# Seven-product matrix blocks in the last layer of a four-layer forward pass, with edits at the joins of its stages

## The reference

```python
proj = h @ w_in[l]
rq, rk, rv, rg, mq, mk, mv, ga, gb = jnp.split(proj, split_points, axis=-1)
rq = rotary(rq.reshape(B, S, RET_HEADS, RET_DK), pos)
rk = rotary(rk.reshape(B, S, RET_HEADS, RET_DK), pos) * (RET_DK ** -0.5)
rv = rv.reshape(B, S, RET_HEADS, RET_DV)
ret = jax.nn.silu(rg) * retention(rq, rk, rv)
a = ret @ w_ret_out[l]
mq = rmsnorm_3(mq.reshape(B, S, MOBA_HEADS, MOBA_DH), q_norm_w[l])
mk = rmsnorm_3(mk.reshape(B, S, MOBA_HEADS, MOBA_DH), k_norm_w[l])
b = moba_attention(mq, mk, mv) @ w_moba_out[l]
mix = jax.nn.sigmoid(ga) * a + jax.nn.sigmoid(gb) * b
x = x + mix @ w_o[l]
h2 = rmsnorm_3(x, norm2_w[l])
f = (jax.nn.silu(h2 @ w_ffn_gate[l]) * (h2 @ w_ffn_up[l])) @ w_ffn_down[l]
x = x + f
```

## Time and profile before

| | us |
|---|---|
| median of 3 runs | 2074.97 |
| lowest, highest | 2073.9, 2077.7 |
| profiled execution, whole | 2080.29 |
| its span, first to last instruction | 2078.5 |
| PE (matmul) busy | 2051.6 (99%) |
| PEld (weight load) busy | 1849.7 (89%) |
| DVE busy | 968.5 (47%) |
| POOL busy | 609.2 (29%) |
| ACT busy | 409.6 (20%) |
| DMA, mean share of 16 engines | 41.5% |

### The profile page before, as it was taken

The page is one execution under the profiler, slowest core; times in us unless marked ns, Lnnn a source line. Parts: engine busy times, 40 slices in busy tenths (PEclk is TensorE's granted clock), DMA queues, the critical chain, the costliest instruction groups (busy, mean ns, idle before and its releaser), DMA issues.

```text
span 2078.5 us, 33422 instructions
## 1 busy us (share of the span) xinstructions
PE 2051.6 (99%) x12602; PEld 1849.7 (89%) x12602; DVE 968.5 (47%) x2568; ACT 409.6 (20%) x993; POOL 609.2 (29%) x418
## 2 busy tenths in 40 slices
PE   8999999999999999999999999999999999999998
PEld 6778789888889999999888888999998888889998
DVE  4144436973353566614982354556811033324451
ACT  2231521112111222111111112032202114210000
POOL 1000033000001487855000000567770000008782
PEclk9999999999999999999999999999999999999999
DMA  5304444343344454444443333444444432344543
GB/s 203 127 27 139 140 142 162 128 142 121 122 142 142 142 183 163 156 153 159 148 140 122 128 136 122 169 156 169 172 168 142 142 122 82 124 159 166 174 160 132
DMA packets 42310, 297.39 MB, mean 143 GB/s; under 512 B 4800, under 2 KB 4928, under 8 KB 8512
## 3 DMA queue, kind: packets, MB, share of 16 engines
q1 hardware_dynamic: 42176, 295.55, 41.5%
HBM read 294.48 MB, written 1.05 MB: 142 GB/s over the span
## 4 chain that ended last, share of the span: by engine, by line
PE 55%; DVE 2%; POOL 1%; ACT 1%; issue 0%; ACTq 0%; DVEq 0%; POOLq 0%
PE bank L698 54%; DVE xn L1639 0%; PE bank L697 0%; DVE tmp L1623 0%; DVE arena L2027 0%; ACT arena L1215 0%; POOL h_res L1587 0%; POOL h_res L1594 0%; POOL h_res L1597 0%; POOL h_res L1585 0%; DVE bank L1618 0%; DVE arena L1950 0%; DVE arena L1943 0%; DVE arena L2022 0%; DVE arena L2024 0%
## 5 line engine op out<-in xcount | busy, mean ns | idle before, releaser
L698 PE MATMUL bank<-xn,ring 128*128 128x256 f32 (+3 forms) x4064 | 779.3, 351 | 0.6 <-DMA ring<-wstream 0.6
L698 PEld LDWEIGHTS bank<-xn,ring 128*128 128x128 f32 (+1 forms) x4064 | 685.6, 190 | 84.8 <-issue 3.7
L698 PE MATMUL bank<-arena,ring 128*128 128x128 f32 (+3 forms) x3606 | 652.4, 337 | 12.8 <-DMA ring<-wstream 10.0
L698 PEld LDWEIGHTS bank<-arena,ring 128*128 128x128 f32 x3606 | 569.6, 191 | 79.2 <-DMA ring<-wstream 10.3
L698 PE MATMUL bank<-arena 128*128 128x128 f32 (+5 forms) x1912 | 258.5, 291 | 1.0 <-ACT arena L1184 1.0
L698 PEld LDWEIGHTS bank<-arena 128*128 128x128 f32 (+2 forms) x1912 | 233.7, 192 | 13.6 <-issue 5.5
L1184 ACT ACTIVATE arena<-bank 128x256 f32 (+6 forms) x268 | 106.9, 402 | 666.3 <-PE bank L698 554.2
L1585 POOL TENSOR_TENSOR h_res<-ring 128x512 f32<-128x512 f32 x9 | 11.4, 1272 | 751.8 <-DMA ring<-wstream 671.6
L1618 DVE SCALAR_TENSOR_TENSOR arena<-arena,par (+2 forms) x536 | 214.5, 477 | 0.4 <-DVE arena L2084 0.2
L698 PE MATMUL bank<-arena,h_res 128*128 128x128 f32 x1616 | 193.7, 276 | 2.9 <-DVE arena L2027 1.2
L698 PEld LDWEIGHTS bank<-arena,h_res 128*128 128x128 f32 x1616 | 186.1, 192 | 5.3 <-POOL h_res L1594 2.0
(11 more groups left out here) (207 smaller groups left out, 1520.5 us busy)
## 6 DMA issues: line engine op xcount, KB each, us to landing
ring<-wstream SPq DMA_DIRECT2D x262, 1024.0 KB, 4.8
ring<-wstream SPq DMA_DIRECT2D x15, 768.0 KB, 4.2
cst<-consts SPq DMA_DIRECT2D x1, 2616.0 KB, 15.1
ring<-wstream SPq DMA_DIRECT2D x4, 512.0 KB, 3.7
h_res<-tokens SPq DMA_DIRECT2D x2, 544.0 KB, 5.3
out<-arena SPq DMA_DIRECT2D x1, 1024.0 KB, 4.1
ring<-wstream SPq DMA_DIRECT2D x2, 384.0 KB, 3.2
ring<-wstream SPq DMA_DIRECT2D x2, 288.0 KB, 2.8
```

The costliest lines, as they stand in the source:

```text
L698: return pe.matmul(o, lhs, rhs, start=start, stop=stop, skip_group_check=True)
```

## The change

Twenty-two plain blocks of C become seven-product blocks: two of `mqk`, two of `mv`, four each of `rqk`, `rv` and `rg`, and three of four each of `ret` and `o` (the first of these two stay plain as `ret0`, `o0`). Token sums for `xn`, `retn` and `mg3` are new work for DVE, and POOL mixes 22 more blocks. The gate of retention is now formed in SBUF (`gate_of_retention`), and the rotation of C's queries and keys moves to between the `rv` blocks on PE, and to after `rv` 1, 2, 3 and `rg` 0 on DVE. `mv` and `rv` come out token by token, so weights and activations change places in their matmuls.

Besides: `A.qr` becomes one block, `B.rg` two of 1 MB (written out, no loop). The wait for A's values moves from ahead of the head loop to the first head's output. The last head of A's attention moves into the first block of `A.out`, the last head of C's into the first block of `C.moba`. The first block of `B.out` is cut in two halves of k. Twelve matmul instructions on zeros, whose result nobody reads, stand at the very start. The down product pairs neighbouring row tiles, 2k and 2k + 1, in L0, L1 and C, and the sums come after hidden pairs 3, 7, 9 and 10. The transpositions and stores of the result go out in four groups, three of them inside `C.down` and `C.down3`.

```diff
     pl("C.mqk0", "w_in_3", 0, 1, 2, 8, seq(3072))
-    pl("C.mqk", "w_in_3", 0, 1, 2, 8, seq(3584))
-    pl("C.mv", "w_in_3", 0, 1, 2, 8, seq(4096))
-    pl("C.rqk", "w_in_3", 0, 2, 2, 8, seq(0))
-    pl("C.rv", "w_in_3", 0, 2, 2, 8, seq(1024))
-    pl("C.rg", "w_in_3", 0, 2, 2, 8, seq(2048))
+    fast("C.mqk", "w_in_3", 0, 2, 1, lambda it, q: 3584 + 256 * it)
+    fast("C.mv", "w_in_3", 0, 2, 1, lambda it, q: 4096 + 256 * it)
+    fast("C.rqk", "w_in_3", 0, 4, 1, lambda it, q: 256 * it)
+    fast("C.rv", "w_in_3", 0, 4, 1, lambda it, q: 1024 + 256 * it)
+    fast("C.rg", "w_in_3", 0, 4, 1, lambda it, q: 2048 + 256 * it)
     pl("C.gate", "w_in_3", 0, 4, 2, 8, seq(4608))
     pl("C.moba", "w_moba_out_3", 0, 1, 2, 4, lambda it, q: span(512 * q, 512))
-    pl("C.ret", "w_ret_out_3", 0, 2, 2, 8, seq(0))
-    pl("C.o", "w_o_3", 0, 2, 2, 8, seq(0))
+    pl("C.ret0", "w_ret_out_3", 0, 1, 1, 8, seq(0))
+    fast("C.ret", "w_ret_out_3", 0, 3, 1, lambda it, q: 256 * it + 256)
+    pl("C.o0", "w_o_3", 0, 1, 1, 8, seq(0))
+    fast("C.o", "w_o_3", 0, 3, 1, lambda it, q: 256 * it + 256)
...
-
...
@@ -681,10 +688,11 @@
                 if stage == "A.lat1":
                     sp.dma_start(par[:, ND:], params[:, ND:]).then_inc(params_in, 16)
...
+                sp.wait_ge(*e.at(("out", g)))
+                sp.dma_start(out[0].rearrange("(n p) d -> p n d", p=P)[:, :, S * g:S * g + S],
+                             out_sb[:, :, S * g:S * g + S]).then_inc(stored, 16)
+            sp.wait_ge(stored, 64)
 
 
...
+            def turned_out(g, events):
+
+                e.turn["side"] += e.turn["side"] % 4 == 0
+                b = e.take("side", ("out", g))
+                pe.wait_ge(*e.emptied(("out", g)))
+                for j in range(2):
+                    pe.wait_ge(*e.at(("C", "x", events[j % len(events)])))
+                    for t in range(2):
+                        ins = mm(b, slice(0, P), slice(S * t + P * j, S * t + P * j + P), x_res[:, 2 * g + j, P * t:P * t + P],
+                                 C("ident"), transpose=True)
+                ins.then_inc(*e.side_done(("out", g)))
...
+                        if L == "C" and (it, r) >= (1, 1) and r == 1:
+                            turned_out(it - 1, [it - 1])
                         held = fast_block((L, "down", it, r), (L, "down", it),
-                                          lambda h, k, t: hidden[:, 11 * h + ks[k], P * t:P * t + P], (L, "down", r),
+                                          lambda h, k, t: hidden[:, 2 * ks[k] + h, P * t:P * t + P], (L, "down", r),
...
+            for n in range(6):
+                mm(7, slice(0, P), slice(0, S), sq[:, 8, 0:P], sq[:, 8, 0:S])
             raw = lambda k: xg_a[:, k, :]
...
-            output1(MLA_H - 1)
-            out_product("A.out", lambda k: y1[:, k, :], TA, ready=[("y1", h) for h in range(MLA_H)])
+
+            def last_head():
+
+                turned1(last)
+                output1(last - 1)
+
+            out_product("A.out", lambda k: y1[:, k, :], TA, ready=[("y1", h) for h in range(MLA_H)],
+                        split=[(range(5), last_head), (range(5, 6), lambda: output1(last)), (range(6, 8), None)])
...
-            blocks("B.rg", 2, None, TA, tiles=4)
+            for i in range(2):
+                slot = e.next_block()
+                pe.wait_ge(*e.landed(slot))
+                w = ring[:, slot, :].rearrange("p (q k c) -> p q k c", q=2, k=2)
...
             blocks("B.g1", 8, xk(TA), TA)
-            out_product("B.out", lambda k: yb[:, k, :], TA, ready=[("yb", j) for j in range(ND)])
+            out_product("B.out", lambda k: yb[:, k, :], TA, ready=[("yb", j) for j in range(ND)],
+                        split=[(range(4), None), (range(4, 8), None)])
...
-            blocks("C.rqk", 8, x256, S)
+            fast_stage("C", "mqk", 2, 1, of_tokens(xn), ("C", "x"), normed("C.n1"))
+            fast_stage("C", "mv", 2, 1, of_tokens(xn), ("C", "x"), None, token_major=True)
+            fast_stage("C", "rqk", 4, 1, of_tokens(xn), ("C", "x"), None)
             pe.wait_ge(*e.at(("C.mqk", "sq", 7)))
             row_sums("C.mqk", 8, "pick64", 2)
-            blocks("C.rv", 8, x256, S, token_major=(0, 1))
+            values, gates = ((lambda its, part=part, tm=tm: [
+                fast_block(("C", part, it, 0), ("C", part, it, 0), of_tokens(xn), ("C", "x"), token_major=tm)
+                for it in its]) for part, tm in (("rv", True), ("rg", False)))
+            values((0, 1))
+            for p in (0, 2, 1, 3):
+                for part in ("c11", "c12", "c22"):
+                    pe.wait_ge(*e.at((("C", "rqk", p, 0), part)))
+                swapped("C.rot", p, "ret.swap", rqk0)
+            values((2, 3))
+            gates((0, 1))
             row_spread("C.mqk", 4, 2)
-            blocks("C.rg", 8, x256, S)
-            for p in (0, 2, 1, 3):
-                pe.wait_ge(*e.at(("C.rqk0", 1, 1)))
-                swapped("C.rot", p, "ret.swap", rqk0)
+            gates((2, 3))
...
-            causal_heads(e, pe, mm, "C.", 8, lambda h: mqk[64 * (h % 2):64 * (h % 2) + 64, h // 2, :],
-                         lambda h: mqk[64 * (h % 2):64 * (h % 2) + 64, 4 + h // 2, :],
-                         lambda h, t: mv[:, t, 64 * h:64 * h + 64], gate_block, retention, pair=True)
-            for event in [("C.mo", h) for h in range(8)]:
...
+            for q in range(2):
+                halves("C.moba", q, 4, [P] * 4, lambda k: mo[:, k, :], S,
+                       ready=None if q else [("C.mo", 2 * k + 1) for k in range(4)],
+                       split=None if q else [(range(2), lambda: output(7)), (range(2, 4), None)])
             for h in range(4):
                 pe.wait_ge(*e.at(("C.retn", h)))
-            blocks("C.ret", 8, lambda k: retn[:, k, :], S)
-            out_product("C.o", lambda k: mg3[:, k, :], S, ready=merged("C.ret"))
+            halves("C.ret0", 0, 8, [P, P], lambda k: retn[:, k, :], S)
+            fast_stage("C", "ret", 3, 1, of_tokens(retn), ("C", "retn"), None)
+            halves("C.o0", 0, 8, [P, P], lambda k: mg3[:, k, :], S,
+                   ready=[("C.ret0", "m", 0, t) for t in range(2)] + [("C", "m", k // 2) for k in range(6)], late=2)
+            fast_stage("C", "o", 3, 1, of_tokens(mg3), ("C", "mg"), None)
...
             for r, (k0, nk) in enumerate(down_rows):
+                if r == 1:
+                    turned_out(2, [2])
                 held = halves("C.down3", 0, nk, [P, P], lambda k: hf3[:, k0 + k, :], S,
...
+            turned_out(3, [3, 4])
...
-                if block[1:] in (("up", 0, 0), ("a", 0, 0)):
+                if block[1:] in (("up", 0, 0), ("a", 0, 0), ("mqk", 0, 0)):
...
-                for r, ks in enumerate(DOWN_PAIRS):
-                    if it + 1 == (7, 9, 10)[r]:
+                for r, first, n in ((0, 0, 4), (1, 4, 4), (2, 8, 2), (2, 10, 1)):
+                    if it + 1 == first + n - 1:
...
+            for j in range(ND):
+                dve.wait_ge(*e.at(("C.n1", "xn", j)))
+            token_sums(("C", "x"), xn)
...
+            def rotated(p):
+
+                rotate_pair("C.rot", p, rqk, rqk0, "ret", ("C.rqk", p))
+
+            for it in range(4):
+                unite(("C", "rv", it, 0), rv, S * it, token_major=True)
+                if it >= 1:
+                    rotated((0, 2, 1)[it - 1])
+            unite(("C", "rg", 0, 0), rg[:, 0:2, :], 0)
+            rotated(3)
+            unite(("C", "rg", 1, 0), rg[:, 2:4, :], 0)
             spread_norm("C.mqk", 4, lambda p: "q_norm_w_3" if p < 2 else "k_norm_w_3", mqk0, mqk, "C.mqkn")
-            with e.turns("C.rg", 2) as i:
...
-            for p in (0, 2, 1, 3):
-                rotate_pair("C.rot", p, rqk, rqk0, "ret", ("C.rqk", p))
-
+            for it in (2, 3):
+                gate_of_retention(it - 2)
+                unite(("C", "rg", it, 0), rg[:, 2 * it:2 * it + 2, :], 0)
```

288 lines of the change are left out of this document (166 added, 122 removed).

## The result

| | us |
|---|---|
| kernel before, median of 4 runs in this comparison | 2076.34 (2073.9 to 2080.95) |
| kernel after, median of 4 runs | 2049.19 (2048.46 to 2052.29) |
| ratio, 95% interval | 0.987 (0.9848 to 0.9891) |
| profiled execution of after, and its span | 2048.46, 2046.6 |
| profiled execution of before, and its span | 2080.29, 2078.5 |

Forecast: 2046, range 2041 to 2056. The interval of the ratio lies wholly under 1. The medians differ by 27.2 us, the two profiled executions by 31.8 (31.9 in span), the forecast was 29.1. Why these three are not the same is the main question of what follows.

What follows compares the result with a forecast made beforehand. The prediction took PE's own work as the bound, matmuls filling 99% of the span. Its terms, 15.0 us from C's 22 blocks and the rest from joins, summed to 29.1, taken from the median 2074.97: 2046 us, range 2041 to 2056.

Steps and rivals of the forecast that it cites:

- The 22 blocks: C's plain blocks become seven-product blocks, 6.25 us instead of 6.93 each: 15.0 us less on PE.
- the reserve: In C's projection, `unite` on DVE may lag by about 4.6 us before PE waits for it.
- no lag to speak of: DVE in C's rotation blocks: operations beside mixes average 1.8 us, 6.3 per block against 6.25; cost taken as 0.
- The steps of the single waits: Gains at short waits: `A.qr` 1.9 us, `B.rg` 1.1, A's values 1.0, C's last head 0.6, its first 0.5.
- The end: End of the program: transpositions and stores in groups leave less behind the last matmul, 2.2 us (0.5 to 2.8).
- The sum before `down`: In L0, the last sum, now of one pair, is done before the mix: 1.2 us (0 if another operation meets it).
- The start: Twelve idle instructions before the first load may raise PE's clock: 0 to 2.8 us, taken as 1.4.
- PE's work shrinks by an amount that hardly depends on the run: Whole program: reason for subtracting the 29.1 us from the median 2074.97, not from the profiled 2080.3.
- The end of A's attention: Matmuls of `A.out` fill PE's 1.74 us gap and the clock should not fall: 4.6 us (2.5 if it falls).
- DVE falling behind: Rival in `rv` and `rg`: all four rotations meet mixes at the worst, PE waits; about 2053 us, chance 0.13.
- Slot refill: Rival in C's blocks: mixes wait for each other and DVE, 8.4 us per block; 2093 us, chance 0.03.
- The joins giving less: Rival: clock low at start and A's end, `down` still waits, store 1 us longer; 2052 us, chance 0.12.

Runs made afterwards that it cites:

- experiment 4: Kernel after with down's pairs of hidden columns as before (halves 11 apart, sums of 4, 4 and 3 pairs): 2050.11 us (2048.62 to 2052.65).
- experiment 2: Kernel after without the six idle matmuls (12 instructions) ahead of the first load, and without their zeroing by POOL: 2050.87 us (2049.3 to 2051.3).
- experiment 1: Kernel after with the end of A's attention as before, A.out beginning after output 7: 2053.99 us (2051.18 to 2055.1).
- experiments 2 to 12: Kernels made from after, each with a part undone, changed or added, the last with three edits together; measured medians from 2042.13 to 2053.87 us.
- experiments 7 and 8: Kernel after with one, or three dependent, extra DVE additions behind each `unite` of `rv`; spans 2046.8 and 2052.5 us against 2046.6.
- experiment 8: Kernel after with three extra DVE additions, each waiting for the one ahead, behind each `unite` of `rv`; span 2052.5 us against 2046.6.

## Why the forecast was right, and where it was not

**The 22 blocks: right.** 6.25 us each, 15.6 measured for all of C up to `up` against 15.7, and six blocks made plain gave 3.9 of 4.1 back. DVE beside the mixes: 1.8 for a mean operation and 6.26 for a block stood in the trace as computed, and the reserve was 5.0 against 4.6. What I had called "no lag to speak of" is right, yet nearer to the edge than it reads: DVE has no idle time in three of these blocks.

**The steps of the single waits: right within 0.5.** `A.qr` gave 2.4 for 1.9, B 1.6 for 1.1. A part may be what a restart after a wait costs beside the wait itself; no run tells this apart. The end gave 2.6 for 2.2, the transfer's size being worth 2.0, not 1.7. With it goes the one sign that did not come: the last matmul of `C.down3` ends 3.9 us before the end (2042.7 of 2046.6), not 4 to 5.

**The sum before `down`: the number right, the reason not borne out.** L0 and L1 gave 1.0 for 1.2, but the reason, the shorter last sum, did not show in experiment 4: the old pairing ran without the wait too. The delay by a mix is real. With the change it stands in `up`, 0.5 in the profiled execution and up to 1.7 in those of the kernels made from it, a term that my sum did not have. Why it stood ahead of `down` in before is open.

**The start: mis-sized.** 1.4 was the middle of what I had left open. Where the clock held it was 2.8 (2.6 undone by experiment 2). But in three of the twelve traces that have the idle matmuls the next 32 instructions took 9.2 to 9.3 us instead of 7.6, with a PE gap of 2.0 to 2.3 us ahead of them; in the other nine the gap was 0.9 to 1.7 us. One of the three, and its windows:
```profile
1.11 4.31 PE L704 MATMUL bank<-sq 128*128 128x256 f32 x12 [1.11 <-POOL small L1599]
7.49 9.28 PE L704 MATMUL bank<-arena,ring 128*128 128x272 f32 x32 [2.07 <-DMA ring<-wstream]
```
```profile
7.00:10.00 3.00, 2.51 (x6) 1.93 (x7) 1.13 (x4) 1.13 (x4) 1.79 (x3) 0.58 1.06 431
10.00:14.00 4.00, 4.00 (x17) 3.26 (x16) 0.55 (x1) 0.26 (x1) 1.15 (x2) 0.89 1.07 452
```
On average over the twelve it gives 2.8 - 1.7 x 3/12 = 2.4. In these three the twelve idle instructions took 4.3 to 4.5 us, in the nine 4.9 to 5.5: they ran faster and so ended earlier, which made the gap longer. More idle matmuls, up to the load, would close it; this wasn't tried.

**The step that failed: "PE's work shrinks by an amount that hardly depends on the run, so I subtract from the median".** 2046 is 3.2 us under the 2049.2: 1.4 by the base and 1.9 by the gain. What the runs showed in place of an amount that is the same in each run:
- The end of A's attention is worth 4.75 only against an execution in which the clock fell, as in the profiled one of before. Of 24 further executions of before, 12 had a mean clock of 0.998, with a median of 2078.0 us; 9 had 0.999 (2075.5) and 3 had 1.0 (2074.7). Where the clock fell in them no trace shows. That it was mostly behind this gap is argued from counts: with the gap (these 24 and the four of experiment 1) 14 of 28 had 0.998, without it (after and the eight kernels of experiments 2 to 12 that were timed several times) 1 of 38. By that, some 2.7 us are not there to be gained in about half the executions, 1.3 on average, an estimate.
- The start gives 0.4 less on average than in the traces compared.
- The wait in `up` averages 0.8 us over the eleven traces from after on with the sums in one piece, 0.3 more than in after's.
- All this takes the 31.9 of the traces to 29.9. The measured 27.2 has an interval of about 4.5 us either way. The profiled execution of before took 2080.3, 2.3 above the median of executions at its clock; what those 2.3 are its trace can't tell, since there is no second trace of before beside it. That part stays open. Against the median of the 24 further executions, 2076.8, the gain is 27.6.
- And the 2074.97 shown ahead of the forecast was a median of three; over the comparison it was 2076.3, which put the forecast 1.4 too low by itself.
- That 29.1 came so near 27.2 is in part luck: the sum was 2.8 short of what the traces show (1.4 of it the start), and the traces show 4.7 more than the medians. The two errors run against each other.

**The rivals.** DVE falling behind: its condition was met (every rotation met a mix), its price not, for the reason shown in experiments 7 and 8. Slot refill: the blocks stayed at 6.25. The joins giving less: true of the clock in some executions, and it decides some microseconds between executions; the 2052.29 of after (mean clock 0.999) may be such a case, which no trace shows.

## What to carry to other kernels

When one engine is solid for 99% of the time, count its work from start to start of like blocks and take the joins one by one: that held within 0.1 us for 15.7. But ask of each term whether it stands in every execution; a term that contains a fall of the clock behind a short gap, or an operation that happens to meet another engine's step, is worth its share of the executions, and it is to be taken off the typical run, not off the traced one. And where an operation of one engine is held up by a step of another, count how many operations meet a step, since each was held for what was left of one (all of them here had 512 columns; no run varied that). Spread them over the blocks instead of placing four in a row: that removed the wait in `up`.

## What the hardware showed that I had not expected

- The same gap of 1.73 to 1.74 us in front of the same work left the clock at 1.00 in one execution and took it to 0.50 in another (the earlier trace rows against experiment 1). A fall behind a short gap cost 1.7 us (start), 2.0 (experiment 8) and 3.0 (4.75 - 1.74, end of A's attention in before).
- In the first microseconds of the program the clock column says 1.00 while a matmul of 272 columns takes twice its later time (experiment 2). There the pace has to be read, not the column.
- The second and third step of a mix take 1.25 us in the mean, but 1.60 when an operation of DVE with two SBUF inputs runs as it starts, against 1.27 with DVE out of the way: the meeting costs both sides, 0.33 us for POOL, as its rows under experiments 7 and 8 show.
